# Two more places for expert weights, interleaved first gathers, and a last unit in two transfers

## The reference

```python
def expert_choice_ffn(h, w_router, b_router, w_gate, w_up, w_down):
    aff = jax.nn.softmax((h @ w_router + b_router).astype(jnp.float32), axis=-1)
    gate, idx = lax.top_k(jnp.swapaxes(aff, 1, 2), cap)            # cap = 32
    xe = jax.vmap(lambda hb, ib: hb[ib])(h, idx)
    hid = jax.nn.silu(jnp.einsum("becd,edf->becf", xe, w_gate)) * jnp.einsum("becd,edf->becf", xe, w_up)
    ye = jnp.einsum("becf,efd->becd", hid, w_down) * gate[..., None].astype(h.dtype)
    # scatter-add of ye to the picked rows; then h + gate2 * moe, and rms_norm(h) * final_norm_g
```

## Time and profile before

| | us |
|---|---|
| median of 3 runs | 1272.88 |
| profiled execution | 1270.42 |
| its span on the core | 1268.6 |
| TensorE busy | 1059.8 (84%) |
| chain that ended last, TensorE's share | 60% |
| chain that ended last, DMA's share | 28% |

### The profile page before, as it was taken

The page is one execution under the profiler, slowest core; times in us unless marked ns, Lnnn a source line. Parts: engine busy times, 40 slices in busy tenths (PEclk is TensorE's granted clock), DMA queues, the critical chain, the costliest instruction groups (busy, mean ns, idle before and its releaser), DMA issues.

```text
span 1268.6 us, 17835 instructions
## 1 busy us (share of the span) xinstructions
PE 1059.8 (84%) x7574; PEld 580.6 (46%) x7574; DVE 432.5 (34%) x1048; ACT 227.0 (18%) x554; POOL 64.0 (5%) x73
## 2 busy tenths in 40 slices
PE   6899999999999999999988979887666666666665
PEld 2344764444585458875677864532111111112111
DVE  0127646433766445354147664411000000010001
ACT  0012144101214423432111231210000000000001
POOL 0101000000000000002213400000000000000000
PEclk9999999999999999899988989899888989888898
DMA  9963338443247952113110015699999999999995
GB/s 383 373 254 133 124 129 337 150 160 133 115 166 310 428 224 84 67 66 135 68 68 2 4 43 194 249 413 432 430 429 429 429 431 430 430 429 430 429 429 238
DMA packets 24847, 323.66 MB, mean 255 GB/s; under 512 B 2897, under 2 KB 3025, under 8 KB 5441
## 3 DMA queue, kind: packets, MB, share of 16 engines
q1 hardware_dynamic: 22736, 314.18, 60.4%
q0 software_dynamic: 2032, 8.35, 1.9%
HBM read 321.47 MB, written 1.05 MB: 254 GB/s over the span
## 4 chain that ended last, share of the span: by engine, by line
PE 60%; DMA 28%; DVE 7%; issue 3%; ACT 2%; POOL 0%; SPq 0%; DVEq 0%; ACTq 0%; POOLq 0%
PE banks L610 49%; DMA ring<-in_stream 16%; DMA Vt_to_O<-in_stream 7%; PE banks L621 3%; DMA zuv_to_Kt<-in_stream 2%; DMA QKT<-in_stream 2%; PE banks L2127 2%; PE banks L871 1%; PE banks L857 1%; DVE Vt_to_O L2397 1%; PE banks L892 1%; PE banks L854 1%; PE banks L758 1%; DVE probs L1215 1%; DVE KC L1207 0%
## 5 line engine op out<-in xcount | busy, mean ns | idle before, releaser
L610 PE MATMUL banks<-ring,uT 128*128 128x512 f32 (+1 forms) x512 | 226.1, 597 | 8.5 <-DMA ring<-in_stream 4.6
L610 PEld LDWEIGHTS banks<-ring,uT 128*128 128x128 f32 x512 | 96.4, 192 | 122.7 <-issue 114.1
L610 PE MATMUL banks<-ring,scr 128*32 128x512 f32 (+1 forms) x656 | 108.3, 665 | 39.2 <-DMA ring<-in_stream 38.9
L2611 DVE SCALAR_TENSOR_TENSOR UWK<-UWK,banks 128x256 f32<-128x256 f32 x16 | 6.7, 421 | 281.3 <-ACT UWK L2868 281.3
L610 PE MATMUL banks<-ring,UWK 128*32 128x512 f32 (+1 forms) x368 | 87.6, 744 | 17.8 <-DMA ring<-in_stream 11.7
L610 PE MATMUL banks<-scr 64*64 64x64 f32 (+2 forms) x2048 | 82.4, 234 | 7.1 <-DVE scr L2445 5.2
L610 PEld LDWEIGHTS banks<-scr 64*64 64x64 f32 (+1 forms) x2048 | 79.2, 144 | 12.8 <-issue 6.1
L610 PEld LDWEIGHTS banks<-ring,scr 128*32 128x32 f32 (+1 forms) x656 | 29.2, 124 | 111.1 <-DMA ring<-in_stream 59.3
L2127 PE MATMUL banks<-UWK 128*128 128x512 f32 x128 | 58.7, 601 | 23.7 <-DVE UWK L2621 23.7
L2868 ACT ACTIVATE UWK<-banks 128x256 f32<-128x256 f32 x16 | 6.1, 383 | 379.8 <-PE banks L610 379.8
L610 PE MATMUL banks<-UWK,ring 128*128 128x256 f32 x320 | 72.5, 387 | 0.0
(11 more groups left out here) (365 smaller groups left out, 1197.2 us busy)
## 6 DMA issues: line engine op xcount, KB each, us to landing
ring<-in_stream SPq DMA_DIRECT2D x106, 2048.0 KB, 16.3
QKT<-in_stream SPq DMA_DIRECT2D x14, 2048.0 KB, 30.8
Vt_to_O<-in_stream SPq DMA_DIRECT2D x14, 2048.0 KB, 30.9
zuv_to_Kt<-in_stream SPq DMA_DIRECT2D x14, 2048.0 KB, 30.8
w<-in_w POOLq DMA_DIRECT2D x2, 1024.0 KB, 9.5
probs<-in_rows POOLq DMA_DIRECT2D x4, 512.0 KB, 5.4
const<-in_consts SPq DMA_DIRECT2D x1, 1135.0 KB, 22.0
resid<-in_x SPq DMA_DIRECT2D x1, 1024.0 KB, 14.1
```

The lines of the kernel that those rows point to most:

```text
L610: return pe.matmul(o, a, b, start=start, stop=stop)
```

## The change

- **Two more places.** `EXTRA = 5`. Slots 7 and 8 are made of two pieces of 8 KB a partition each (1 MB a transfer), so a unit there comes in two DMAs, and both count on one semaphore. Slot 7 is the whole of `wide` and the end of `scr` with the start of `qk`; slot 8 is the later part of the constants and the front of the new tile `misc` (which now holds `par`, `rowsp` and `modrows`). To make room the constants are put in another order, and `scr` and `QKT` become one tile `scr_qk`.
- **When they are filled.** Slot 4 is moved by 1024 floats and now waits for `G_mm 1,1`, a product in the middle of the mixer's chunks. Slot 7 waits for the last token rows (`h_lat 1,1`), slot 8 for `grow_mm 1,1`. They stand behind the first fill of the seven others, as units 59 and 60. Unit 61 waits for `gu_mm 0,0`, and from there each unit waits for the one nine before it.
- **First products between the gathers.** Banks 0 and 1 of the first products come ahead of the experts, banks 2 and 3 behind the first and the second `gu` unit. ScalarE now takes banks 0 and 2, VectorE 1 and 3, and VectorE's `Pg` and `grow` work moves behind or between them.
- **Last unit in two transfers.** Unit 147 comes as two DMAs of 1 MB. The second has a semaphore of its own (`arrived_last`), and TensorE waits for it ahead of the third of the four row blocks.
- **Combination by halves.** TensorE waits for `ye` half 0, does its two products, then waits for half 1.
- `fin_row` is loaded behind the last gather (`xe_mm 7`) rather than behind the logits; `Pone` and `fin_row` lie elsewhere.

Eight of the 16 first products (128x128) have moved behind expert 0's first and second unit; nothing is added. The diff, cut to its core:

```diff
-EXTRA = 3
+EXTRA = 5
+SPLIT = (RING + 3, RING + 4)
...
-    cycle = late[0:2] + list(range(RING, RING + EXTRA)) + late[2:]
+    cycle = late[0:2] + list(range(RING, SPLIT[0])) + late[2:] + list(SPLIT)
...
-        par = sb("par", P_COLS)
+        misc = sb("misc", P_COLS + R_SMALL + 512)
+        par, rowsp, modrows = (misc[:, lo:hi] for lo, hi in ((0, P_COLS), (P_COLS, P_COLS + R_SMALL),
+                                                             (P_COLS + R_SMALL, P_COLS + R_SMALL + 512)))
...
-        more = (qk[:, 0:UNIT], Vt_to_O[:, :], zuv_to_Kt[:, :])
+        HALF = UNIT // 2
+        more = (qk[:, 1024:1024 + UNIT], Vt_to_O[:, :], zuv_to_Kt[:, :])
+        C_LATE = CF["upto"][0]
+        pieces = ((wide[:, :, :].rearrange("p t d -> p (t d)"), scr_qk[:, 4096:4096 + HALF]),
+                  (const[:, C_LATE:C_LATE + HALF], misc[:, 0:HALF]))
...
                 elif slot[k] == RING:
-                    sp.wait_ge(*at("QS_mm", 3, 1))
+                    sp.wait_ge(*at("G_mm", 1, 1))
+                elif slot[k] == SPLIT[0]:
+                    sp.wait_ge(*at("h_lat", 1, 1))
+                elif slot[k] == SPLIT[1]:
+                    sp.wait_ge(*at("grow_mm", 1, 1))
                 elif slot[k] > RING:
                     sp.wait_ge(*at("mix2", 1, 1))
-                sp.dma_start(held(slot[k]), A["stream"][k, :, :]).then_inc(*tick(f"arrived{slot[k]}", by=16))
+                if k == len(units) - 1 or slot[k] in SPLIT:
+                    for i, half in enumerate(halves(slot[k])):
+                        sem = "arrived_last" if (k, i) == (len(units) - 1, 1) else f"arrived{slot[k]}"
+                        sp.dma_start(half, A["stream"][k, :, i * HALF:(i + 1) * HALF]).then_inc(*tick(sem, by=16))
+                else:
+                    sp.dma_start(held(slot[k]), A["stream"][k, :, :]).then_inc(*tick(f"arrived{slot[k]}", by=16))
...
                     ins.then_inc(*fill(6, "gu_mm", e, i))
+                    if e == 0 and i < 2:
+                        pe_gather_first(pe, i + 2)
...
+                        if (e, i, q) == (EXPERTS - 1, 1, 2):
+                            pe.wait_ge(K.sem("arrived_last"), 16)
...
-                pe.wait_ge(*at("ye", e, 0))
-                pe.wait_ge(*at("ye", e, 1))
-                for t in range(TILES):
-                    for h in range(2):
+                for h in range(2):
+                    pe.wait_ge(*at("ye", e, h))
+                    for t in range(TILES):
...
-            for t in range(TILES):
-                dve.tensor_tensor(Pg[:, t, :, :], Pone[:, t, :, :], over(aff[:, t, :], CAP), ALU.mult).then_inc(*tick("vector_step", "Pg"))
-            v_grow(dve, 1)
-            for b in (0, 2):
+            def rows(b):
...
+            rows(1)
+            for t in range(TILES):
+                dve.tensor_tensor(Pg[:, t, :, :], Pone[:, t, :, :], over(aff[:, t, :], CAP), ALU.mult).then_inc(*tick("vector_step", "Pg"))
+            rows(3)
+            v_grow(dve, 1)
...
-            for b in (1, 3):
+            for b in (0, 2):
                 act.wait_ge(*at("xe0_mm", b))
...
-            pool.wait_ge(*at("route_mm"))
+            pool.wait_ge(*at("xe_mm", DCH - 1))
```

More of the change, by code:

```diff
@@ L78 @@
 CF, C_COLS = fields([
-    ("ident", P), ("spread", 32), ("ones", P), ("upto", P), ("before", P), ("same", P), ("cumf", P), ("cumb", P), ("iota", CAP),
+    ("ident", P), ("spread", 32), ("ones", P), ("iota", CAP), ("eps", 2),
+    ("upto", P), ("before", P), ("same", P), ("cumf", P), ("cumb", P),
     ("tri64", 2 * CH), ("neg64", 2 * CH), ("id64", CH), ("level", LEVELS * 2 * CH),
     ("cos64", TILES * 32), ("sin64", TILES * 32), ("cos32", TILES * 16), ("sin32", TILES * 16),
-    ("causal", P), ("cmpneg", TILES * N_CMP), ("cmpok", TILES * N_CMP), ("eps", 2)])
+    ("causal", P), ("cmpneg", TILES * N_CMP), ("cmpok", TILES * N_CMP)])
 PF, P_COLS = fields([
@@ L188, in slots @@
     late = early[first:first + RING]
-    cycle = late[0:2] + list(range(RING, RING + EXTRA)) + late[2:]
+    cycle = late[0:2] + list(range(RING, SPLIT[0])) + late[2:] + list(SPLIT)
     slot = [early[k] if k < first else cycle[(k - first) % len(cycle)] for k in range(len(order))]
-    use, before, seen = [], [], {}
+    use, before, seen, parts = [], [], {}, {}
     for k, b in enumerate(slot):
         past = seen.setdefault(b, [])
-        use.append(len(past) + 1)
+        parts[b] = parts.get(b, 0) + (2 if b in SPLIT and k < len(order) - 1 else 1)
+        use.append(parts[b])
         before.append(past[-1] if past else None)
@@ L398, in build @@
         two = ExitStack()
[L400 to L403, removed]
+        scr_qk = sb("scr_qk", 5120 + QKV_BLOCKS * TOK2, stack=two)
+        flat, qk = scr_qk[:, 0:5120], scr_qk[:, 5120:5120 + QKV_BLOCKS * TOK2]
+        scr = flat.rearrange("p (t a n) -> p t a n", t=2, a=5)
         QT = qk[:, 0:H2 * SEQ].rearrange("p (b n) -> p b n", n=SEQ)
@@ L464, in build @@
         selT = uwk[:, 2304:2560]
-        fin_row = uwk[:, 3072:4096]
+        fin_row = uwk[:, 0:1024]
         ye = uwk[:, 4096:6144].rearrange("p (a d) -> p a d", a=2)
-        more = (qk[:, 0:UNIT], Vt_to_O[:, :], zuv_to_Kt[:, :])
+        HALF = UNIT // 2
[3 more added lines that the diff above has]
+                  (const[:, C_LATE:C_LATE + HALF], misc[:, 0:HALF]))
         aff = low(TILES, EXPERTS)
@@ L486, in held, with halves @@
             return ring[:, b, :] if b < RING else more[b - RING]
+        def halves(b):
+            return pieces[SPLIT.index(b)] if b in SPLIT else (held(b)[:, 0:HALF], held(b)[:, HALF:UNIT])
         unit_at = [0]
@@ L494, in take, with take_halves @@
             pe.wait_ge(K.sem(f"arrived{slot[k]}"), 16 * use[k])
+            if slot[k] in SPLIT:
+                return halves(slot[k])
             return held(slot[k])[:, 0:DCH * n].rearrange("p (k n) -> p k n", n=n)
+        def take_halves(pe):
+            k = unit_at[0]
+            take(pe)
+            return halves(slot[k])
         @block.sync
@@ L2049, in pe_route, with pe_gather_first @@
             pe.wait_ge(*at("Pone", "first"))
[L2050 to L2053, removed]
+            for b in range(2):
+                pe_gather_first(pe, b)
+        def pe_gather_first(pe, b):
+            pe.wait_ge(*free(b))
+            for m in (2 * b, 2 * b + 1):
                 for t in range(TILES):
```

23 lines of the change are left out of this document (11 added, 12 removed).

## The result

| | before | changed | ratio, 95% interval |
|---|---|---|---|
| first comparison, median of 4 and 4 runs | 1273.43 | 1259.55 (1256.92 to 1261.42) | 0.9893, 0.9868 to 0.9919 |
| second comparison, 17 and 6 runs | 1272.12 | 1262.25 (1258.8 to 1267.79) | 0.9932, 0.9904 to 0.9959 |
| span of the profiled execution | 1268.6 | 1259.6 | |

The change gained 14 us by the first comparison's medians and 10 by the second's. The forecast was 1261.4, range 1258.5 to 1267.5: right. What follows asks which of its terms were.

A forecast was written before the change was run, and what follows sets the result against it. The prediction took the DMA transfer of expert weights to bound the last third of the kernel. Terms -9.8 - 0.5 + 0 + 0.5 - 1.7 = -11.5 took 1272.9 to 1261.4 us, range 1258.5 to 1267.5.

The forecast's parts named there:

- Two places, -9.8: Ahead of the gapless weight stream: units 59 and 60 land in the idle gap, -9.8 us, bounds 0 and -9.8.
- First products and expert 1, -0.5: At expert 0's start: unit 61 issued some 2.2 us earlier, mostly lost at unit 67; -0.5 us, bounds -0.9 and +1.5.
- Transfers, +0.5: In the gapless stretch: 19 more transfers from units split into 1 MB pieces cost +0.5 us, bounds 0 and 2.8.
- `fin_row`, 0: Beside the stream near 836 us: its 512 KB load is covered by the head start; 0, bounds 0 and +1.2 us.
- Tail, -1.7: Behind the last landing: only 8 of unit 147's instructions are left, -1.7 us, bounds -2.5 and +1.7.
- The combination's 0: In the tail: waiting for `ye` by halves starts TensorE 0.6 us earlier, but ScalarE's squares leave 0 of it.
- the signs: Trace checks: landings at 802 to 813 us, unit 67 near 852.5, pace 4.89, last landing near 1244, tail 12.6 us.
- B: Rival at expert 0, up to unit 67: the interleaving puts TensorE 4 us later, median 1265.4; chance 0.12.
- A: Rival in the gapless stretch: each of 19 extra transfers loses 1.0 us of DMA time, +7, 1280; chance 0.07.
- E: Rival in the gapless stretch: split units make the pace 2% worse on every unit, 8 us, 1269.4; chance 0.04.
- D: Rival at the gap ahead of the stream: only one place works, half of 9.8 is lost, 1266.3; chance 0.07.
- C: Rival at expert 1 and the tail: whole 2.2 us head start kept, higher tail clock gives 0.8, 1258.9; chance 0.12.

## Why the prediction was right

1. **Two places, -9.8.** Right. Both pairs landed by 814.3, and 80 units were left behind unit 67 where 82 had been behind unit 65: 2 x 4.893. One place alone gave 4.57, the second 4.30; what is missing from 4.89 is mostly term 3.
2. **First products and expert 1, -0.5.** The mechanism was right, the size zero. Unit 61 left 1.8 us earlier; unit 67 landed at 83.63, where 65 had at 83.68. The forecast let 0.9 of the head start survive and took 0.4 for the slower expert 0. That cost was 0.7 (75.03 to 75.71). The kernel with expert 1's products moved ahead shows that this place was worth 2.4 us.
3. **Transfers, +0.5.** About right: 0.8 as worked out from the kernel with every unit in two transfers, and the pace rose from 4.893 to 4.904, 0.9 over 80 units. The prediction puts the rule against this edit too strictly. The Trainium skill ("DMA: Bandwidth & Descriptors", section on bandwidth) advises 1 MiB or more a DMA, which the new transfers of 128 x 2048 floats just meet, and its table is of DMAs that GpSimd issues, not SyncE; the table and the fixed 2 us spoke against the edit, the rule did not.
4. **`fin_row`, 0.** Right, with its upper bound: 0 where it stands, 1.26 in the open.
5. **Tail, -1.7.** The size is right by chance: 14.26 - 12.80 = 1.46. The step that failed is "What is left behind the last landing is 8 instructions: 3.44 / 2 = 1.7 us saved". Eight instructions of two row blocks take as long as sixteen of four. What changed in the profile was the clock, 0.5 until +3.0 before and until -1.7 after. With the clock low until +3.1, the kernel with two transfers has a tail of 14.63. At one clock the term is about -0.1. The other 1.3 or so came with the clock, and whether the change brings that is open: there is one profile of the kernel before, and the kernel without the places, whose last landing is within 0.2 us of it, had its clock up 0.2 us ahead of the landing. The combination's 0 was right.

Together: -9.0 in the last landing (-9.8 + 0.9, and nothing from expert 0) and -1.5 in the tail, -10.4; forecast -11.5. With the tail at one clock it would be -9.1. The medians' -13.9 and -9.9 lie on both sides, by the front's scatter. So two terms that were off, 0.5 us that didn't come and a tail gained in another way, leave the total within 1.1 us of the forecast, and that is partly luck.

Of the signs, those up to unit 67's landing, the pace and the tail came as named once the 1.44 us by which unit 55 is later are taken off; the last landing is at 1245.4 by that clock, where 1244 was named. The start of expert 1 at 844.60 is past the 844 that was to speak for B, but it is 843.2 on the clock of the kernel before. One reading of the rows was off, without a consequence: the 27th slice is at 413 GB/s, and the 28th to the 39th are at 429 to 432.

Of the rivals, A and E fell with the pace, D with the kernel with one place. B's mechanism was there with 0.7 us and no loss at the landing. C, that more is kept, was wrong for the changed kernel in its first part. Its second part, the higher clock in the tail, is what the profile shows, and the first median, 1259.55, lies under the forecast's 1259.8 and near C's 1258.9. C's premise, TensorE's part up to expert 1 made shorter, is what the moved products do.

## What to carry to other kernels

Where a stream is the limit, count how many of its units are in when it starts to run without a gap: each place that can be filled earlier is worth one unit's transfer, and a head start that meets a later wait is worth nothing until that wait moves as well. Split the last transfer so that each part uses all of the output's partition blocks, by output columns and not by rows of the weights. Compare traces from a common event near the change, and tails only at the same granted clock.

## What the runs showed of the hardware

**SyncE's queue takes about ten transfers.** With seven places each issue takes 0.33 us. With nine (two of them in two transfers) SyncE stands in it. The issues of one line, between 900 and 1220 us before and between 900 and 1200 now (duration ns min/median/max):

```profile
L514 SPq DMA_DIRECT2D ring<-in_stream x37: 327/328/328, 902.6 to 1207.7; - x37
```

```profile
L541 SPq DMA_DIRECT2D ring<-in_stream x27: 327/2091/8368, 904.9 to 1187.5; - x27
...
DMA to landing us min/median/max: 36.1/40.2/43.0
```

Of the 97 issues from 850 us on, 53 take over 1 us. Counted at the end of each issue between 900 and 1220 us there are 9.8 transfers issued and not landed on average in the changed kernel, at most 11, of 1 or 2 MB; with all units in two transfers 10.4, at most 12, of 1 MB each; before 6.9. With one place of the two there are at most 9, and no issue takes over 0.44 us. So the limit is in transfers, not in bytes. No rate is lost by it (the engines move 429 and 427 GB/s), but here more places or smaller pieces would not make the queue deeper. The places paid by filling the gap ahead of the stream, not by depth.

**The clock at the end.** In seven of the fourteen profiles the granted clock is still at 0.5 at the last landing, in the other seven it has risen 0.2 to 1.7 us before it; with the last unit in two halves by rows the tail is 12.8 there, and 13.1 to 13.3 with the clock at 0.5 until +0.5 to +1.0. It is not the scatter from run to run that was expected with the kernel whose last unit is whole. In the six profiles with the last landing at 475.6 to 476.0 (the changed kernel twice, first products ahead, last unit whole, by columns, both halves wait) the clock rose 1.2 to 1.7 us before it, and in the three with expert 1's products moved ahead 0.8 us behind it. What decides it stays open: three matmuls put in from 0.3 us ahead of the last landing on, where TensorE had no idle time, didn't change it.
